# The even layer's input projection as one stage: x turned and split once and kept on chip, queries, keys and values by block, pool input and gates as channel strips

## The reference, cut to what matters

```python
def pool_mix(u, buf, start, w_pool, scale):      # 512 channels, groups of 128, windows 2, 4, 8, 16
    ...
        win = end[..., sl] - csum[:, POOL_BUF + 1 - w:POOL_BUF + 1 - w + L, sl]
        cnt = jnp.minimum(pos + 1, w).astype(f32)[None, :, None]
        outs.append(win / cnt - cur[..., sl])
    d = jnp.stack(outs, axis=2)
    y = jnp.einsum('blgc,gcd->blgd', d, w_pool.astype(f32)).reshape(B, L, P)
    return y * scale.astype(f32)

def even_layer(h, start, pool_buf, k_past, v_past, norm_g, w_in, w_pool, pool_scale, q_g, k_g, sb_bias, w_out):
    proj = rms_norm(h, norm_g) @ w_in            # 1024 -> 512 u, 512 q, 512 k, 512 v, 1024 gate
    u, q, k, v, gate = jnp.split(proj, [i1, i2, i3, i4], axis=-1)
    pool_y = pool_mix(u, pool_buf, start, w_pool, pool_scale)
    q = rms_norm(q.reshape(B, L, SB_HEADS, SB_HEAD_DIM), q_g)
    k = rms_norm(k.reshape(B, L, SB_HEADS, SB_HEAD_DIM), k_g)
    ...
    mix = jnp.concatenate([pool_y, sb.reshape(B, L, SB_WIDTH)], axis=-1) * jax.nn.silu(gate.astype(f32))
    y = h + mix.astype(h.dtype) @ w_out
```

## Time and profile before

| | us |
|---|---|
| median of 3 runs | 3413.97 |
| lowest and highest of them | 3411.51, 3418.04 |
| the profiled execution | 3415.91 |
| span of its profile | 3414.3 |
| stage A (0 to about 387) | 387 |
| stage Q (to 762.2) | 375.2 |
| stage C (1239.5 to 1692.2) | 452.7 |

### The profile page before, as it was taken

How to read it: one execution, slowest core, us unless ns; L and a number is a source line. 1 busy time by engine, 2 the same in 40 slices (tenths; PEclk the granted TensorE clock), 3 DMA queues, 4 the chain that set the end, 5 groups by cost and what they waited for, 6 DMA issues and landing times. The chain is left out here.

```text
span 3414.3 us, 55510 instructions
## 1 busy us (share of the span) xinstructions
PE 3070.2 (90%) x20296; PEld 2660.5 (78%) x20296; DVE 1571.3 (46%) x2417; ACT 1250.6 (37%) x2922; POOL 897.4 (26%) x1225
## 2 busy tenths in 40 slices
PE   7999699968999969999699999999949999995799
PEld 5888488857888857765499999999738999994487
DVE  2111233337888853431165555541037776753322
ACT  3222222218999953432132111211135565550100
POOL 0000023325666631122000000000047667652000
PEclk8999799988999989999899999999959999996799
DMA  4111323336303237788532212222134454432443
GB/s 139 49 49 51 113 77 111 120 94 158 88 22 70 48 122 245 237 281 304 176 117 75 75 61 71 75 76 75 42 103 112 118 133 118 109 83 71 143 143 114
DMA packets 384946, 381.36 MB, mean 112 GB/s; under 512 B 82295, under 2 KB 300672, under 8 KB 380611
## 3 DMA queue, kind: packets, MB, share of 16 engines
q1 hardware_dynamic: 370303, 342.55, 33.8%
q0 software_dynamic: 10240, 33.56, 3.1%
q10 hardware_dynamic: 4192, 2.50, 0.3%
...
## 5 line engine op out<-in xcount | busy, mean ns | idle before, releaser
L1708 PE MATMUL D_ps_y<-D_xT_hi,D_w_hi 128*128 128x416 f32 x1280 | 452.8, 354 | 9.2 <-DVE D_xT_lo L1844 9.2
L1709 PE MATMUL D_ps_y<-D_xT_lo,D_w_hi 128*128 128x416 f32 x1280 | 449.0, 351 | 0.0
L1710 PE MATMUL D_ps_y<-D_xT_hi,D_w_lo 128*128 128x416 f32 x1280 | 448.6, 350 | 0.0
L830 DVE TENSOR_TENSOR_SCAN B_left<-B_ps_z,B_left,B_one 128x512 f32<-128x512 f32 (+3 forms) x272 | 289.7, 1111 | 19.2 <-ACT B_ps_z L791 16.9
L875 POOL TENSOR_TENSOR B_a<-B_take,B_left 128x512 f32<-128x512 f32 (+3 forms) x272 | 255.7, 958 | 140.6 <-PE B_ps_a L743 83.1
L1708 PEld LDWEIGHTS D_ps_y<-D_xT_hi,D_w_hi 128*128 128x128 f32 x1280 | 240.5, 188 | 11.8 <-issue 9.3
L1710 PEld LDWEIGHTS D_ps_y<-D_xT_hi,D_w_lo 128*128 128x128 f32 x1280 | 240.6, 188 | 3.2
L1709 PEld LDWEIGHTS D_ps_y<-D_xT_lo,D_w_hi 128*128 128x128 f32 x1280 | 241.2, 188 | 2.0
L789 ACT ACTIVATE B_take<-B_ps_z,B_bias 128x512 f32<-128x512 f32 (+3 forms) x320 | 208.4, 652 | 25.7 <-PE B_ps_z L733 18.5
L728 PE MATMUL B_ps_z<-B_qk 128*128 128x128 f32 (+3 forms) x928 | 192.2, 339 | 26.8 <-DVE B_bias L816 26.0
L1508 POOL MEMSET G_ones<- 128x128 f32 x1 | 0.2, 205 | 786.0 <-POOLq L147 786.0
...
## 6 DMA issues: line engine op xcount, KB each, us to landing
...
scratch_turned<-Q_turned SPq DMA_DIRECT2D x17, 1024.0 KB, 5.9
C_pg<-in_cache_k POOLq DMA_DIRECT2D x64, 256.0 KB, 3.8
C_pg<-in_cache_k SPq DMA_DIRECT2D x64, 256.0 KB, 3.3
C_pg<-in_cache_v SPq DMA_DIRECT2D x64, 256.0 KB, 4.4
C_pg<-in_cache_v POOLq DMA_DIRECT2D x64, 256.0 KB, 4.2
...
```

The costliest lines, as they stand in the source:

```text
L830: dve.tensor_tensor_scan(buf[:, hh, at:at + w][:, ::-1], p_z[n % Z][:, 0:w][:, ::-1], one[:, 0:1].to_broadcast([P, w]), buf[:, hh, at + w: ...
L1708: pe.matmul(dst, w_hi[:, slot, k, :], xT_hi[:, k, cols], start=(k == 0), stop=False)
L1709: pe.matmul(dst, w_hi[:, slot, k, :], xT_lo[:, k, cols], start=False, stop=False)
L1710: mm = pe.matmul(dst, w_lo[:, slot, k, :], xT_hi[:, k, cols], start=False, stop=(k == KC - 1))
```

## The change

The two runs of `stage_a` become one. ACT scales a tile of x by `rstd` before it is turned; `xT_hi` and `xT_lo` now hold all 2080 tokens, turned and split once. The stage has two phases:

- 51 items, block by block (q, then k, then v; `project(i)`): 17 tiles each, 24 matmuls of 512 columns an item, the weights in a ring of 12 chunks that is refilled meanwhile (`chunks_at`). The heads of q and k are normed, turned, split and stored as before, one block of 512 at a time, from one buffer `turned` by two transfers of 256 KB (`store_turned`).
- 12 strips of 128 channels (`strip(s)`): u and gate of the groups 0 to 3 in turn, then gates 4 to 7. In a strip the weights are stationary and 416 tokens move, in five blocks, 24 matmuls a block. u stands by channel, so the windows are sums of u with itself shifted by 1, 2, 4, 8 tokens on DVE (`windows`), and the only product left on PE is the one by `w_pool` (`mix`), five a group, woven into the strip after next. The mix is stored by channel to `mixT`.

Stage C loads `mixT` as it is and has no `turn_mix`; the sample tile runs with 32 rows in place of 128. The tensor `gd` of the odd layer is no longer allocated during A to C.

```diff
--- before.py
+++ after.py
...
-def stage_a(nc, io, cat, heads):
...
+def stage_a(nc, io, cat):
...
+        NTT = NT + 1
+        TOK = SEQ + NS
+        NB = 5
+        BT = TOK // NB
+        LP = SEQ - (NB - 1) * BT
+        RING, SRING = 12, 3
+        UNITS = 3 * KC
+        ITEMS = 3 * NTT
+        QKI = 2 * NTT
+        PAD = BUF
+        STRIPS = [(kind, g) for g in range(NG) for kind in "ug"] + [("g", g) for g in range(NG, 2 * NG)]
+        NST = len(STRIPS)
+        xT_hi, xT_lo = (sb(n, [P, KC, TOK], F32R) for n in ("xT_hi", "xT_lo"))
...
+        p_y, p_m = p_x + p_pj, p_t
...
+        def strip_w(s):
+            return (w_low[:, s % SRING * 2 + i, :].rearrange("p (k c) -> p k c", k=KC) for i in range(2))
...
+            def store_turned(i):
+                b, t = divmod(i, NTT)
+                m = rows_of(t)
+                sp.wait_ge(s_hi2, i + 1)
+                sp.wait_ge(s_lo2, i + 1)
+                for a, part in ((0, 1 if b else 3), (1, 2 if b else 0)):
+                    sp.dma_start(io["turned"][:, :, part, t * P:t * P + m], turned[:, a, :, 0:m].bitcast(F32)).then_inc(s_to, 16)
...
+            def turn_x(t):
+                m = rows_of(t)
+                pe.wait_ge(s_xn, t + 1)
+                if t > 0:
+                    pe.wait_ge(s_xlo, 2 * t)
                 for k in range(KC):
+                    mm = pe.transpose(p_x[k // 4][:, k % 4 * m:(k % 4 + 1) * m], x[0:m, t % 2, k * P:(k + 1) * P], ident[0:m, 0:m])
                 mm.then_inc(s_xp, 1)
...
+            def project(i):
+                b, t = divmod(i, NTT)
+                m = rows_of(t)
+                if b == 0:
+                    pe.wait_ge(s_xlo, 2 * t + 2)
+                if i >= 3:
+                    pe.wait_ge(s_ev, i - 2)
+                out, cols = p_pj[i % 3][0:m, :], slice(t * P, t * P + m)
+                for k in range(KC):
+                    if t == 0:
+                        pe.wait_ge(s_wlo, KC * b + k + 1)
+                    hi, lo = chunk(KC * b + k)
+                    pe.matmul(out, xT_hi[:, k, cols], hi, start=(k == 0), stop=False)
+                    pe.matmul(out, xT_hi[:, k, cols], lo, start=False, stop=False)
+                    mm = pe.matmul(out, xT_lo[:, k, cols], hi, start=False, stop=(k == KC - 1))
+                    if t == NT and k < KC - 1:
+                        mm.then_inc(s_free, 1)
+                mm.then_inc(s_pj, 1)
...
+            def turn_hist(g):
+                if g == 0:
+                    pe.wait_ge(s_pin, 32)
+                else:
+                    pe.wait_ge(s_ro, 2 * g)
+                n = DB * BUF
+                pe.transpose(p_r[:, 2 * P:2 * P + n], buf_in[0:n, g * P:(g + 1) * P], ident[0:n, 0:n]).then_inc(s_ht, 1)
...
+            def turn_rows(g):
+                pe.wait_ge(s_yev[NB - 1], 2 * g + 1)
+                pe.wait_ge(s_hist, g + 1)
+                pe.transpose(p_r[0:BUF, 0:P], u[:, PAD + SEQ - BUF:PAD + SEQ], ident[:, :])
+                pe.transpose(p_r[0:NS, P:2 * P], u_s[:, :], ident[:, :]).then_inc(s_r, 1)
...
+            def mix(g, n):
+                if n == 0:
+                    pe.wait_ge(s_ch, steps_before(g + 1))
+                    if g == 0:
+                        pe.wait_ge(s_lo2, QKI)
+                if NB * g + n >= 2:
+                    pe.wait_ge(s_m, NB * g + n - 1)
+                last = win[(WIN[g].bit_length() - 2) % 2]
+                pe.matmul(p_m[(NB * g + n) % 2][:, 0:BT], w_pool[:, g, :], last[:, PAD + n * BT:PAD + (n + 1) * BT],
+                          start=True, stop=True).then_inc(s_mm, 1)
...
+            def strip(s):
+                kind, g = STRIPS[s]
+                if kind == "u":
+                    turn_hist(g)
+                pe.wait_ge(s_slo, s + 1)
+                hi, lo = strip_w(s)
                 for n in range(NB):
+                    if s > 0:
+                        pe.wait_ge(s_yev[n], s)
+                    elif n == 0:
+                        pe.wait_ge(s_xlo, 2 * NTT)
+                    elif n >= 2:
+                        pe.wait_ge(s_ev, ITEMS)
+                    dst, cols = p_y[n][:, 0:BT], slice(n * BT, (n + 1) * BT)
                     for k in range(KC):
+                        pe.matmul(dst, hi[:, k, :], xT_hi[:, k, cols], start=(k == 0), stop=False)
+                        pe.matmul(dst, hi[:, k, :], xT_lo[:, k, cols], start=False, stop=False)
+                        mm = pe.matmul(dst, lo[:, k, :], xT_hi[:, k, cols], start=False, stop=(k == KC - 1))
+                    mm.then_inc(s_y[n], 1)
+                    if 2 <= s <= 2 * NG and s % 2 == 0:
+                        mix(s // 2 - 1, n)
...
+            turn_x(0)
+            for i in range(ITEMS):
+                if 1 <= i < NTT - 1:
+                    turn_x(i + 1)
+                project(i)
+                if i == 0:
+                    turn_x(1)
+                if 0 <= i - 2 < QKI:
+                    turn_qk(i - 2)
+            for s in range(NST):
+                strip(s)
...
+            for i in range(ITEMS + 1):
+                if i + 1 < NTT:
+                    x_hi(i + 1)
+                if i + 2 < NTT:
+                    square(i + 2)
+                if i >= 1:
+                    out(i - 1)
+                if 0 <= i - 3 < QKI:
+                    turned_hi(i - 3)
+                if i + 2 < NTT:
+                    scale_x(i + 2)
+                for n in chunks_at(i):
+                    w_hi(n)
...
+            def windows(g):
+                w = WIN[g]
+                levels = w.bit_length() - 1
+                at = steps_before(g)
+                if g == 0:
+                    dve.wait_ge(s_zero, 3)
+                    for i in range(2):
+                        dve.wait_ge(s_vo[i], 16 * (NTT // 2 + (1 - i)))
+                dve.wait_ge(s_ht, g + 1)
+                dve.tensor_copy(ext_s[0][:, :, 0:BUF], p_r[:, 2 * P:2 * P + DB * BUF].rearrange(
+                    "p (b r) -> p b r", r=BUF)).then_inc(s_hist, 1)
                 for n in range(NB):
+                    dve.wait_ge(s_yev[n], 2 * g + 1)
+                dve.tensor_copy(ext_s[0][:, :, BUF:BUF + DS], u_s[:, :].rearrange("p (b t) -> p b t", t=DS)).then_inc(s_new, 1)
+                src, src_s = u, ext_s[0]
+                for n in range(levels):
+                    sh = 1 << n
+                    dst, dst_s = win[n % 2], ext_s[1 + n % 2]
+                    if n > 0:
+                        dve.wait_ge(s_ch, at + 2 * n)
+                    dve.tensor_tensor(dst[:, PAD:PAD + SEQ], src[:, PAD:PAD + SEQ], src[:, PAD - sh:PAD + SEQ - sh],
+                                      ALU.add).then_inc(s_ch, 1)
...
+            for i in range(ITEMS + 1):
+                if i + 1 < NTT:
+                    x_lo(i + 1)
+                if 0 <= i - 1 < QKI:
+                    head_sums(i - 1)
+                if 0 <= i - 3 < QKI:
+                    turned_lo(i - 3)
+                if 0 <= i - 1 < QKI:
+                    heads_normed(i - 1)
+                for n in chunks_at(i):
+                    w_lo(n)
+                if i in (QKI + 6, QKI + 10):
+                    split_strip((i - QKI) // 4 - 1)
+            for s, (kind, g) in enumerate(STRIPS):
+                if s + 2 < NST:
+                    split_strip(s + 2)
+                if 2 <= s <= 2 * NG and s % 2 == 0:
+                    for n in range(NB):
+                        mix_out(s // 2 - 1, n)
+                if kind == "u":
+                    windows(g)
+                elif g < NG:
+                    rows(g)
...
+                sp.dma_start(mix[:, t % 2, :, 0:m], io["mixT"][:, :, t * P:t * P + m]).then_inc(s_mix_in[t % 2], 16)
...
-            def turn_mix(t):
-                pe.wait_ge(s_mix_in[t % 2], 16 * (t // 2 + 1))
-                if t > 0:
-                    pe.wait_ge(s_mlo, 2 * t)
-                if t == NT:
-                    pe.wait_ge(s_xr, 2 * (NT - 1))
-                elif t >= 3:
-                    pe.wait_ge(s_xr, 2 * (t - 2))
-                for k in range(KC):
-                    mm = pe.transpose(p_t[k // 4][:, k % 4 * P:(k % 4 + 1) * P], mix[:, t % 2, k * P:(k + 1) * P], ident[:, :])
-                mm.then_inc(s_mt, 1)
-
...
-                pe.wait_ge(s_mlo, 2 * min(t + 3, NT) if t < NT - 1 else 2 * (NT + 1))
...
-                    turn_mix(t + 1)
...
+                act.activation(mT_hi[:, t % 2, 0:4, 0:m], mix[:, t % 2, 0:4, 0:m], ACT.Copy).then_inc(s_mhi, 1)
...
+    stage_a(nc, io, cat)
+    stage_b(nc, io, cat)
+    stage_c(nc, io, cat)
     with nc.sbuf_tensor("gd", [P, 6, NT + 1, H1], F32) as gd:
-        stage_a(nc, io, cat, heads=False)
-        stage_a(nc, io, cat, heads=True)
-        stage_b(nc, io, cat)
-        stage_c(nc, io, cat)
...
```

(22 more changed lines are left out.)

760 lines of the change are left out of this document (369 added, 391 removed).

## The result

| | before | after |
|---|---|---|
| median | 3412.74 (4 runs) | 3294.97 (4 runs) |
| lowest, highest | 3410.05, 3418.04 | 3292.41, 3297.22 |
| span of the profile | 3414.3 | 3292.6 |
| B's first load | 762.22 | 651.25 |
| C's first load | 1239.5 | 1128.5 |

After stands to before as 0.9653 (95% interval 0.9636 to 0.967). The forecast was 3263, its range 3235 to 3315: the sign and the range hold, and the time is 32 us above the point. The two profiles show where that is. The projection gained 111.0 us in place of 126, stage C (its first load to the first matmul of D's main loop) 4.4 in place of 25. B took 477.3 us both times, as forecast.

The account below looks back on a forecast made before the run. Stages A and Q were taken as bound by PE's queue, stage C by PE with some loss to transfers. Span 3414.3 less 126 (projection) and 25 (stage C) gave 3263 us, range 3235 to 3315.

Parts of the forecast that it names:

- The projection: Everything ahead of B, first phase and strips: B begins at 636.4 in place of 762.2, gain 126 us.
- stage C: Turning the mix and its waits go, and the sample tile shrinks: gain 25 us (15 to 33).
- item 8: Block of the queries: four weight chunks fetched through two raw buffers hold ACT up, 4 us (0 to 8).
- The projection's matmuls, strips, tail: Items 6.93, 6.06, 5.62 us; strips phase 288 us, matmuls 0.187 each; then evacuation 1.1, last megabyte 5.9, seam 0.5.
- The start: First phase: the steady beat begins with item 2 at 35 us (25 to 45).
- Stage C, values and end: Seven value tiles gain 1.0 us each, 7 (0 to 16); the sample tile at 32 rows gains 3 (0 to 5).
- Stage C, keys: Key tile seams: turning the mix and the shared-bank wait go, 2 x 0.8 + 6 x 2.3 = 15.4 us gained.
- 1: First block: ACT's chain sets the beat, items 7.6 us in place of 6.93; kernel 3273 to 3280; chance 0.15.
- 2: Stage C values wholly bound by DMA, smaller pieces a little worse: 3273, with keys also held 3288; chance 0.12.
- 3: Strips: weight loads hide better, matmuls 0.173 us each, 20 us less: 3243; chance 0.09, shared with a start near 25.
- 4: First phase: single buffer `turned` makes turned_hi wait for transfers; 3333 at 8.6 us cycle (0.06), slow end 3535 (0.03).
- several holds together: Whole kernel: start 45, stage C gaining 15 and ACT's chain setting the first block's beat, 3300 to 3320; chance 0.05.

Follow-up runs that it names:

- `best_mix4k`: `best` with `mixT` laid out by token tile, so that stage C reads pieces of 4 KB in place of 512 B; 3261.80 us.
- `best`: Against the changed kernel: m_hi and m_lo later in stage C's tiles, weight chunks refilled singly with later loads, start's waits and order changed; 3262.04 us.
- `strip320`: Against the changed kernel: odd strips multiply 320 tokens a block in place of 416, with the same matmuls and weight loads; 3268.61 us (one run).

## Why the prediction was right, and where 32 us went

The sign and most of the gain came by the mechanism that was forecast, one pass over x and fewer products in PE's queue. That the time lies inside the range is in part its width: two terms were off beyond their own bounds (item 8, 9.8 against 0 to 8; stage C, 4.4 against 15 to 33), and 6.4 us of luck from D on stood against them. In the profiles 15 at B and 20.6 in C, less these 6.4, make 29.2; the remaining 3 are the median of after, which lies 2.4 above the span of its profile where the prediction had the two cancel, and rounding.

- **The projection's matmuls, strips, tail: right.** Items took 6.88, 6.04 and 5.58 us (6.93, 6.06, 5.62). From the first strip (355.44) to the last matmul (645.1) it is 289.7 us, against 288; from there to B's first load 6.1, against 7.5. The other mixing work took 0.69 each (0.72). PE waited 0.57 us three times between rows and history.
- **The start: the term was mis-sized**, 42.2 in place of 35. It was guessed from stage Q's start; nobody asked which loads ACT's first wait names. It named the gain and four constants, of which phase 1 needs two, and those only for its heads.
- **Item 8: mis-sized**, 9.8 in place of 4. The text counted ACT's work on four chunks. Left out were the queue of SP, in which stores and loads of x wait behind loads that wait for DVE, and the fall of the clock after 7 us of idle. With 1.5 for small waits at the seams of the blocks: 7.2 + 5.8 + 1.5 + 1.7 - 1.4 = 14.8, the whole difference at B.
- **Stage C, values and end: right** in size (7.0 and 3.6 against 7 and 3), the values with luck: the same code gives 4.4 to 11.5 in the six profiles.
- **Stage C, keys: the step failed.** "Turning the mix and the wait for the shared bank fill them, and both go" was read from PE's rows alone. What is late next was not asked: the second filling of the two banks, behind the chain over ACT and DVE, which arrived at the same time with or without the turning (7.98 and 7.96 us). The fall of the clock, which took some 6 us more, was not priced at all. Forecast +15.4, measured -3.6 in the key tiles. The start of C lost 2.7 besides (1.3 to 3.3 in the six profiles); what costs it stays open, and 4 KB pieces do not cure it (77.2 in `best_mix4k` against 77.0 in `best`).
- **Rivals.** 1 fell: POOL's pair took 0.19 + 0.54 beside DVE. 2 has its time (3273 to 3288) near the result, but not by its mechanism: keys are not held by DMA. 3 fell: 0.189 and not 0.173; yet the reason given against it ("the weight loads alone fill 393.9 of 400") was wrong too, as `strip320` shows. The Trainium skill ("TensorE: Matmul & The Clock Gate", section "Back-to-back issue gap") gives columns / 2.4 GHz + 2.5 ns for a single matmul by itself. An estimate by it is too short here: 0.176 against the 0.189 measured for 416 columns, and 0.136 against 0.146 for 320. 4 did not happen as a beat: ACT waited for `turned` 23 times, 70.9 us, but PE's items kept their length; the single buffer reached PE only where SP's queue was held up. The case of several holds together, 3300 to 3320 at 0.05, came nearest.
